# Head sums over squares split into two reduced-precision parts, and the hand-over from merge to routing without waits for stores

## The chip, the cores and the metric

The kernel runs on one core of a Trainium2 chip. The core has a matrix engine (TensorE, PE in the tables, with its weight loads as PEld), a vector engine (VectorE, DVE), an activation engine (ScalarE, ACT), a general engine (GpSimd, POOL) and a queue engine (SyncE, SP) that issues most transfers. The metric is the device time of one execution in microseconds; less is better.

## What is computed

One hybrid decoder block over 2048 tokens and 16 learned meta tokens (2064 columns), width 1024. Cut to what the change touches:

```python
xn = rmsnorm(h, norm1_g)
proj = xn @ w_in + b_in
u_conv, q, k, v, f_logit, gate_c, gate_a = split(proj)
y_conv = conformer_conv(u_conv, ...)
q = rmsnorm(q.reshape(B, L, N_HEADS, HEAD_DIM), q_norm_g)   # a sum over 64 channels of each head
k = rmsnorm(k.reshape(B, L, N_HEADS, HEAD_DIM), k_norm_g)
o = forgetting_attention(q, k, v, logf)
merged = sigmoid(gate_c) * y_conv + sigmoid(gate_a) * (o @ w_attn_out)
h = h + merged @ w_out
hn = rmsnorm(h, norm2_g)
h = h + hierarchical_moe(hn, ...)      # routing, then 64 experts of which each token takes 2
```

## The kernel before

The program is five stages, each a block of five instruction lists, one for each engine: project, attend, merge, route, experts. A block ends when every engine has come to its end, and only then does any engine start the next (the branch rows of L1326 and L1818 below are such a turning). All orders are written out by hand; engines wait on semaphores.

**Products in parts.** A matrix product of full-precision operands is made of three products of reduced-precision parts (type F32R): `pair_matmuls` (L92 to L94) multiplies high by high, low by high and high by low. A high part is a rounding copy, a low part the difference, made by an engine that subtracts.

**Project.** `w_in` is taken in tiles of 128 columns. PE makes a tile in five chunks of 412 or 414 of the 2064 columns (`CHUNKS`), 24 matmuls each, into banks 0 to 4. GpSimd splits the weight tile after next into its parts when PE has finished a tile (`split_w`, L396 to L403: a cast L400 and a subtraction L402). After 18 front tiles (convolution and gates) come `N_QK` = 8 tiles of queries and keys, 4 of values, one of the forget gate and further gates. In the 8 tiles of queries and keys each of the 40 chunks needs the mean square of its head: ScalarE reads the bank twice (L642, the scaled copy in `work`; L645, the square in `sq`), PE sums the squares over the channels of a head by a product with `head_ones` (`head_sum`, L501 to L510) after the chunk that follows, ScalarE takes the root (L626), VectorE the reciprocal (L830) and multiplies (L832), ScalarE makes the high part (L632) and VectorE the low part (L821) of the result. `head_ones` and `sq` are full-precision, so a head sum is one instruction, which the trace shows as two records. `sq`, `root` and `inv_root` have two buffers each. The last head sum follows right behind its own chunk (L515 and L516). At the start of the value tiles ScalarE and VectorE wait until all queries and keys are stored (L657, L840).

**Merge.** For each of four groups of 512 columns PE makes 8 products of the convolution and 8 of attention; VectorE gates and adds them (L1559, L1564, L1566) and SP stores each (L1400). In the last group ScalarE and VectorE also split `w_out` into parts, in 8 pieces: VectorE takes pieces 0 to 5 (`OUT_LOWS`, L1656), GpSimd pieces 6 and 7 (L1486 to L1488). SP's list ends with a wait for all eight stores (L1431 and L1432).

**Route.** 16 tiles of 128 tokens. For each, PE multiplies merged rows by `w_out` (48 matmuls), VectorE adds x (L2075), ScalarE and VectorE form the norm, PE turns the tile (L1911). GpSimd first makes eleven constants in a row (L1863 to L1881), and PE's list begins with a wait for the eleventh (L1902), although the first use is the first turning of a tile. Before tile 0 may be added, VectorE has to make `r_lo` (L2068) from what ScalarE makes at L2000, and that waits for five small transfers which SP issues behind the first rows, the gain `norm2_g` last. Rows of merged values for tile 2 are loaded once tile 0 has been added; their low part is L2344.

## Time and profile before

| what | value |
|---|---|
| median of 3 runs | 2595.53 us |
| lowest and highest | 2595.42, 2598.49 us |
| the profiled execution | 2595.53 us |
| its span in the trace | 2593.9 us |
| PE busy | 2450.6 us, 94% |
| DVE busy | 1839.8 us, 71% |
| ACT busy | 1049.9 us, 40% |
| POOL busy | 527.8 us, 20% |

The span is the stretch between the first and the last instruction in the trace; 1.6 us of the execution lie around it. Busy shares are means over stages with different limits, so the stage in question has to be looked at. A row of the timeline gives the start and the length of an instruction in microseconds from the span's start, and in brackets how long its engine had been idle and what ended that. Matmuls are pipelined: one shows as 0.35 us long where the next starts 0.19 us later, so PE's pace is read from starts.

### The profile page before, as it was taken

To read this page: it belongs to the slowest core of one execution; us is meant where nothing else is said; L and a number is where in the kernel's file an instruction comes from. 1 tells how busy PE (TensorE), PEld (TensorE's weight loads), DVE (VectorE), ACT (ScalarE), POOL (GpSimd) and SP (SyncE) were. 2 spreads that over 40 slices of the span, in tenths; PEclk is the share of its full clock that TensorE was granted. 3 is DMA by queue.
4 is the path that set the end of the run, shared out by engine and by line. 5 is a ranking of instruction groups with operands and counts; after the bars stand their busy time and mean duration, and the time that the engine had idled before them with its cause. 6 is when DMAs were issued, how large, how long until landed. Compare 5 with 4: busy or idle time off the path is not lost. (4 is left out here: it accounts for less than half of the span.)

```text
span 2593.9 us, 33454 instructions
## 1 busy us (share of the span) xinstructions
PE 2450.6 (94%) x12296; PEld 2002.8 (77%) x12296; DVE 1839.8 (71%) x2380; ACT 1049.9 (40%) x1516; POOL 527.8 (20%) x478
## 2 busy tenths in 40 slices
PE   6999999999999999999995998999399999999998
PEld 6899898999987878889884776877367767777664
DVE  7699999677211078888886775466588888888773
ACT  6101001443212168778774122233255555555540
POOL 1222222111101101111110001011324444232321
PEclk9999999999999999999998999999699999999999
DMA  5111212232325153364424776446379999999986
GB/s 173 41 57 57 68 54 68 71 123 82 108 103 157 49 149 100 100 171 110 115 82 123 204 224 224 178 148 227 138 293 357 368 375 360 372 370 370 361 315 199
DMA packets 180271, 469.84 MB, mean 181 GB/s; under 512 B 33573, under 2 KB 104579, under 8 KB 145548
## 3 DMA queue, kind: packets, MB, share of 16 engines
q1 hardware_dynamic: 133202, 371.64, 42.1%
q0 software_dynamic: 31120, 49.48, 5.6%
q10 hardware_dynamic: 15794, 46.67, 4.7%
q8 instruction: 96, 1.57, 0.2%
q14 instruction: 59, 0.48, 0.1%
HBM read 408.65 MB, written 118.29 MB: 203 GB/s over the span
## 5 line engine op out<-in xcount | busy, mean ns | idle before, releaser
L92 PE MATMUL project_bank<-project_xnT_hi,project_w_hi 128*128 128x512 f32 (+4 forms) x1352 | 511.3, 378 | 0.8 <-DVE project_work L788 0.7
L93 PE MATMUL project_bank<-project_xnT_lo,project_w_hi 128*128 128x512 f32 (+4 forms) x1352 | 497.4, 368 | 0.0
L94 PE MATMUL project_bank<-project_xnT_hi,project_w_lo 128*128 128x512 f32 (+4 forms) x1352 | 495.4, 366 | 0.0
L801 DVE SCALAR_TENSOR_TENSOR project_work<-project_work,project_taps 128x2048 f32<-128x2048 f32 x128 | 335.4, 2620 | 4.5
L92 PEld LDWEIGHTS project_bank<-project_xnT_hi,project_w_hi 128*128 128x128 f32 (+1 forms) x1352 | 250.6, 185 | 36.0 <-issue 7.7
L93 PEld LDWEIGHTS project_bank<-project_xnT_lo,project_w_hi 128*128 128x128 f32 (+1 forms) x1352 | 250.6, 185 | 32.5 <-issue 6.1
L94 PEld LDWEIGHTS project_bank<-project_xnT_hi,project_w_lo 128*128 128x128 f32 (+1 forms) x1352 | 250.7, 185 | 26.7
L2711 PE MATMUL experts_y_bank<-weights_down,experts_hT 128*128 128x512 f32 x544 | 246.4, 596 | 0.6 <-ACT experts_hT L2764 0.6
L1279 DVE TENSOR_TENSOR attend_pT<-attend_t_bank,attend_pT 128x512 fp32r<-128x512 f32 (+3 forms) x352 | 213.9, 614 | 33.7 <-ACT attend_pT L1213 32.8
L1146 PE MATMUL attend_o_bank<-attend_pT,attend_values 128*128 128x256 f32 x1216 | 225.2, 304 | 6.6 <-DVE attend_pT L1279 6.6
L92 PE MATMUL experts_gu_bank<-weights_high,experts_xT_hi 128*128 128x512 f32 x512 | 215.9, 422 | 6.9 <-DVE weights_low L2354 4.4
L1213 ACT ACTIVATE attend_pT<-attend_t_bank 128x512 fp32r<-128x512 f32 (+3 forms) x352 | 184.6, 540 | 87.3 <-PE attend_t_bank L1132 84.7
L93 PE MATMUL experts_gu_bank<-weights_low,experts_xT_hi 128*128 128x512 f32 x512 | 203.3, 397 | 0.0
L592 ACT ACTIVATE project_work<-project_bank,project_params 128x512 f32<-128x512 f32 x64 | 44.0, 690 | 393.4 <-PE project_bank L94 393.4
L94 PE MATMUL experts_gu_bank<-weights_high,experts_xT_lo 128*128 128x512 f32 x512 | 202.4, 395 | 0.0
L2354 DVE TENSOR_TENSOR weights_low<-weights_room,weights_high 128x2048 fp32r<-128x2048 f32 x86 | 193.0, 2285 | 0.0
L1132 PE MATMUL attend_t_bank<-first_ident,attend_probs 128*128 128x128 f32 x1216 | 191.0, 273 | 0.6 <-DVE attend_pT L1279 0.5
L400 POOL CAST project_w_hi<-project_w_raw 128x1024 fp32r<-128x1024 f32 (+1 forms) x35 | 46.5, 1330 | 706.3 <-PE project_bank L94 706.3
L2711 PEld LDWEIGHTS experts_y_bank<-weights_down,experts_hT 128*128 128x128 f32 x544 | 103.4, 191 | 105.7 <-issue 99.2
L2753 ACT ACTIVATE experts_xT_hi<-experts_x_bank 128x1024 fp32r<-128x1024 f32 x64 | 65.7, 1027 | 274.3 <-PE experts_x_bank L2672 219.2
L1146 PEld LDWEIGHTS attend_o_bank<-attend_pT,attend_values 128*128 128x128 f32 x1216 | 167.8, 190 | 9.2 <-DVE attend_pT L1279 8.6
L2349 ACT ACTIVATE weights_high<-weights_room 128x2048 fp32r<-128x2048 f32 x86 | 164.0, 1909 | 13.2 <-DMA weights_room<-in_w_up_dram 13.1
(316 smaller groups left out, 4624.4 us busy)
## 6 DMA issues: line engine op xcount, KB each, us to landing
weights_down<-in_w_down_dram SPq DMA_DIRECT2D x68, 1024.0 KB
weights_room<-in_w_gate_dram SPq DMA_DIRECT2D x45, 1024.0 KB
weights_room<-in_w_up_dram SPq DMA_DIRECT2D x45, 1024.0 KB
weights_third<-in_w_gate_dram SPq DMA_DIRECT2D x23, 1024.0 KB
weights_third<-in_w_up_dram SPq DMA_DIRECT2D x23, 1024.0 KB
project_w_raw<-in_w_in_dram SPq DMA_DIRECT2D x36, 512.0 KB, 4.2
qk_d<-project_work SPq DMA_DIRECT2D x16, 1032.0 KB, 5.4
gate_d<-project_work ACTq DMA_DIRECT2D x16, 1024.0 KB, 4.2
```

What stands on the lines that cost most here:

```text
L92: pe.matmul(out, lhs[0], rhs[0], start=first, stop=False)
L93: pe.matmul(out, lhs[0], rhs[1], start=False, stop=False)
L94: return pe.matmul(out, lhs[1], rhs[0], start=False, stop=last)
L801: nc.vector.scalar_tensor_tensor(out=work[:, 2, 0:SEQ], in0=work[:, 1, META - 1 + q:META - 1 + q + SEQ], scalar=taps[:, bass.ds(ct, 1), q] ...
L1132: m = nc.tensor.transpose(t_bank[:, j % 3, (t % 4) * P:(t % 4 + 1) * P], probs[:, u % BUF, t * P:(t + 1) * P], ident[:, :])
L1146: m = nc.tensor.matmul(out, values[:, h, t, :], pT[:, j % (LAG + 1), t % 4].rearrange("p k q -> p (k q)"), start=t == 0, stop=t == last)
L1213: nc.scalar.activation(pT[:, j % (LAG + 1), 0:n, 0, :], t_bank[:, j % 3, 0:n * P].rearrange("p (t q) -> p t q", q=P), ACT.Copy)\
L1279: nc.vector.tensor_tensor(pT[:, j % (LAG + 1), 0:n, 1, :], t_bank[:, j % 3, 0:n * P].rearrange("p (t q) -> p t q", q=P), raw(pT[:, j % (LA ...
L2349: nc.scalar.activation(self.high[n % 2][:, cut, :, :].rearrange("p c k n -> p k c n"), self.gate_up_rooms[n % 3][:, :, cut, :], ACT.Copy)\
L2354: nc.vector.tensor_tensor(self.low[n % 2][:, cut, :, :].rearrange("p c k n -> p k c n"), self.gate_up_rooms[n % 3][:, :, cut, :], raw(self ...
L2711: m = nc.tensor.matmul(y_bank[:, b, half, :], hT[:, b, c, :], down_raw[r][:, c, cols], start=c == 0, stop=c == HC - 1)
L2753: nc.scalar.activation(xT_hi[:, b, :, :], x_bank[:, :, :].rearrange("p k (c t) -> p (k c) t", t=P), ACT.Copy).then_inc(x_hi_ready, 1)
```

## The change

1. **Head sums.** ScalarE writes the square twice, in full precision (`sq`) and as its high part (`sq_hi`). GpSimd subtracts (`low_squares`, 40 new instructions on 412 or 414 columns, five ahead of each split of a weight tile), and a head sum is two F32R matmuls with `pair_ones`, over the high and the low part. PE waits for GpSimd's part (`sq_lo_ready`). `sq` and `root` have one buffer now, `inv_root` is gone: the reciprocal is made in place, ScalarE's next square waits for the subtraction, its next root for VectorE's product.
2. **The last head sum** stands between the first and the second chunk of the first value tile.
3. **Start of the value tiles.** VectorE doesn't wait for the stores there, ScalarE waits for them where it first writes in their place.
4. **Merge's end.** SP's waits for the stores go to where they are needed: in route on VectorE (ahead of its first writes in that memory) and on SP ahead of the load of tile 12. VectorE takes piece 6 of `w_out` in merge and piece 7 as its first instruction of route; GpSimd takes none.
5. **Constants.** PE waits for the eleven constants ahead of its first turning of a tile instead of at the start of its list.

Two memory tiles of route (`onehot`, `places`) change places in memory.

```diff
@@ -407,12 +414,22 @@
...
-            for it in range(0, N_QK // 2):
-                for b in range(2):
-                    split_w(it * 2 + (N_FRONT + b), b, it + (N_FRONT // 2 + 1))
-            for it in range(0, N_V // 2):
-                for b in range(2):
-                    split_w(it * 2 + (N_FRONT + N_QK + b), b, it + ((N_FRONT + N_QK) // 2 + 1))
+            def low_squares(n):
+                for i, (at, size) in enumerate(CHUNKS):
+                    g = 5 * n + i
+                    wait(pool, bank_read[i], (N_FRONT if i < 4 else 2 * CT) + n + 2)
+                    if g >= 2:
+                        wait(pool, sum_ready, g - 1)
+                    nc.gpsimd.tensor_tensor(sq_lo[:, g % 2, 0:size], sq[:, 0:size], raw(sq_hi[:, g % 2, 0:size]),
+                                            ALU.subtract).then_inc(sq_lo_ready, 1)
+
+            for n in range(2):
+                split_w(N_FRONT + n, n, N_FRONT // 2 + 1)
+            for n in range(N_QK):
+                low_squares(n)
+                split_w(N_FRONT + n + 2, n % 2, (N_FRONT + n) // 2 + 2)
+            for n in range(2, N_V):
+                split_w(N_FRONT + N_QK + n, n % 2, (N_FRONT + N_QK + n) // 2 + 1)
...
@@ -497,23 +514,19 @@
...
+            def head_sum(g):
+                r, size = g % 2, CHUNKS[g % 5][1]
+                pe.wait_ge(root2_ready, g + 1)
+                pe.wait_ge(sq_lo_ready, g + 2)
+                nc.tensor.matmul(bank[:, 5 + r, 0:size], pair_ones[:, :], sq_hi[:, r, 0:size],
+                                 start=True, stop=False)
+                nc.tensor.matmul(bank[:, 5 + r, 0:size], pair_ones[:, :], sq_lo[:, r, 0:size],
+                                 start=False, stop=True).then_inc(sum_ready, 1)
...
             def pair_tile(it, b):
-                def head_sum(g):
-
-
-                    i, r = g % 5, g % 2
-                    size = CHUNKS[i][1]
-
-                    pe.wait_ge(bank_read[i], it * 2 + ((N_FRONT if i < 4 else 2 * CT) + g // 5 + 2))
-                    pe.wait_ge(root2_ready, it * 10 + (g + 1))
-                    nc.tensor.matmul(bank[:, 5 + r, 0:size], head_ones[:, :], sq[:, r, 0:size],
-                                     start=True, stop=True).then_inc(sum_ready, 1)
-
-                first = isinstance(it, int) and it == 0 and b == 0
-                project(it * 2 + (N_FRONT + b), b, CHUNKS, (it * 2 + (N_FRONT + b), it * 2 + (2 * CT + b)),
-                        between=lambda i: None if first and i == 0 else head_sum(5 * b + i - 1))
-                if isinstance(it, int) and it * 2 + b == N_QK - 1:
-                    head_sum(9)
+                n = it * 2 + b
+                project(N_FRONT + n, b, CHUNKS, (N_FRONT + n, 2 * CT + n),
+                        between=lambda i: head_sum(5 * n + i - 1) if n or i else None)
...
                 project(N_FRONT + N_QK + n, n % 2, CHUNKS, (N_FRONT + N_QK + n, 2 * CT + N_QK + n),
-                        between=(lambda g: turn_values(n - 1, g)) if n else None)
+                        between=lambda g: turn_values(n - 1, g) if n else head_sum(5 * N_QK - 1) if g == 0 else None)
...
@@ -622,8 +635,9 @@
                 def root_of(g):
                     r, size = g % 2, CHUNKS[g % 5][1]
                     wait(act, sum_ready, it * 10 + (g + 1))
-                    wait(act, inv_ready, it * 10 + (g + 1))
-                    nc.scalar.activation(root[:, r, 0:size], bank[:, 5 + r, 0:size], ACT.Sqrt,
+                    if it * 10 + g:
+                        wait(act, qn_ready, it * 10 + g)
+                    nc.scalar.activation(root[:, 0:size], bank[:, 5 + r, 0:size], ACT.Sqrt,
                                          bias=eps[:, 0:1], scale=1.0 / HD).then_inc(root2_ready, 1)
...
@@ -642,7 +656,10 @@
                     nc.scalar.activation(work[:, 0, at:at + size], bank[:, i, 0:size], ACT.Identity,
                                          bias=gain_bias[:, bass.ds(it * 2 + b, 1)],
                                          scale=gain[:, bass.ds(it * 2 + b, 1)])
-                    nc.scalar.activation(sq[:, g % 2, 0:size], bank[:, i, 0:size], ACT.Square,
+                    wait(act, sq_lo_ready, it * 10 + (g + 1))
+                    nc.scalar.activation(sq[:, 0:size], bank[:, i, 0:size], ACT.Square,
+                                         bias=bias[:, bass.ds(it * 2 + (8 + b), 1)])
+                    nc.scalar.activation(sq_hi[:, g % 2, 0:size], bank[:, i, 0:size], ACT.Square,
                                          bias=bias[:, bass.ds(it * 2 + (8 + b), 1)]).then_inc(bank_read[i], 1)
...
             over_pair_tiles(pair_tile)
-            for s in qk_stored:
-                wait(act, s, 16 + 16 * N_QK)
+            wait(act, q_lo_ready, 5 * N_QK + 5)
             wait(act, v_pad_ready, 2)
...
                 if g == 0:
                     wait(act, v_stored[n % 2], n // 2 * 16 + 16)
+                    if n < 2:
+                        wait(act, qk_stored[n], 16 + 16 * N_QK)
                 wait(act, v_turned, 5 * n + g + 1)
...
@@ -825,20 +842,17 @@
                 dve.wait_ge(qk_stored[b], it * 32 + 16)
                 for i, (at, size) in enumerate(CHUNKS):
                     g = 5 * b + i
-                    r = g % 2
                     dve.wait_ge(root2_ready, it * 10 + (g + 3))
-                    nc.vector.reciprocal(inv_root[:, r, 0:size], root[:, r, 0:size]).then_inc(inv_ready, 1)
-                    dve.wait_ge(inv_ready, it * 10 + (g + 3))
+                    nc.vector.reciprocal(root[:, 0:size], root[:, 0:size]).then_inc(inv_ready, 1)
+                    dve.wait_ge(inv_ready, it * 10 + (g + 1))
                     nc.vector.tensor_tensor(work[:, 0, at:at + size], work[:, 0, at:at + size],
-                                            inv_root[:, r, 0:size], ALU.mult).then_inc(qn_ready, 1)
+                                            root[:, 0:size], ALU.mult).then_inc(qn_ready, 1)
...
             over_pair_tiles(pair_tile)
-            for s in qk_stored:
-                dve.wait_ge(s, 16 + 16 * N_QK)
             dve.wait_ge(q_lo_ready, 5 * N_QK + 5)
...
@@ -1428,8 +1442,6 @@
                 wait(sp, s, 32)
             next_weights.load_merged(sp, merged_d, 0, 0)
             chunk(TC - 1, False, False)
-            for s in m_stored:
-                wait(sp, s, 16 + 16 * TC)
...
@@ -1483,9 +1495,6 @@
         def _(pool):
             wait(pool, next_weights.merged_hi_ready, 1)
             next_weights.low_merged(nc.gpsimd, 0)
-            for k in range(OUT_LOWS, DC):
-                wait(pool, next_weights.out_hi_ready, k + 1)
-                next_weights.low_out(nc.gpsimd, k, next_weights.out_lo_ready2)
...
-OUT_LOWS = 6
+OUT_LOWS = 7
...
                 sp.dma_start(halves[:, k * size:(k + 1) * size], empty).then_inc(table_cleared, 16)
             for n in range(2, NT):
+                if n == NT - NT // TC:
+                    for s in first_weights.merged_stored:
+                        wait(sp, s, 16 + 16 * TC)
                 load_tile(n, n % 2)
-            wait(sp, r_lo_ready, OUT_LOWS + 1)
+            wait(sp, r_lo_ready, DC + 1)
...
 
         @block.tensor
         def _(pe):
-            pe.wait_ge(consts_ready, 11)
-
             def turn(c, j):
 
                 n = c * CHUNK + j
+                if n == 0:
+                    pe.wait_ge(consts_ready, 11)
                 pe.wait_ge(hn_ready, n + 1)
                 if n < NT - 1:
...
             def low_m(c, j):
                 wait(dve, m_hi_ready, c * CHUNK + (j + 1))
                 first_weights.low_merged(nc.vector, j % 2)
+
+            for k in range(OUT_LOWS, DC):
+                wait(dve, first_weights.out_hi_ready, k + 1)
+                first_weights.low_out(nc, k)
+            for s in first_weights.merged_stored:
+                wait(dve, s, 16 + 16 * TC)
```

On PE, between the second and third chunk of the first tile of queries, before (`project_extra` holds `sq`):

```order
L94 MATMUL project_bank<-project_xnT_hi,project_w_lo 128x412
L509 MATMUL project_bank<-project_extra,project_head_ones 128x412 [waits project_root2_ready,project_bank_read1]
L92 MATMUL project_bank<-project_xnT_hi,project_w_hi 128x414 [waits project_bank_read3]
L93 MATMUL project_bank<-project_xnT_lo,project_w_hi 128x414
L94 MATMUL project_bank<-project_xnT_hi,project_w_lo 128x414
```

and now:

```order
L94 MATMUL project_bank<-project_xnT_hi,project_w_lo 128x412
L521 MATMUL project_bank<-project_squares,project_pair_ones 128x412 [waits project_sq_lo_ready,project_root2_ready]
L523 MATMUL project_bank<-project_squares,project_pair_ones 128x412
L92 MATMUL project_bank<-project_xnT_hi,project_w_hi 128x414 [waits project_bank_read3]
L93 MATMUL project_bank<-project_xnT_lo,project_w_hi 128x414
L94 MATMUL project_bank<-project_xnT_hi,project_w_lo 128x414
```

One full-precision instruction became two, and the wait is for GpSimd's part instead of ScalarE's read of the bank. On GpSimd nothing stood between two splits of weight tiles before; at the same place of the program there is now (`project_squares` holds both parts of the squares):

```order
L423 TENSOR_TENSOR project_squares<-project_extra,project_squares 128x414 [waits project_sum_ready,project_bank_read4]
L407 CAST project_w_hi<-project_w_raw 128x1024 [waits project_tile_done,project_w_loaded0]
L409 TENSOR_TENSOR project_w_lo<-project_w_raw,project_w_hi 128x1024 [waits project_w_hi_ready]
L423 TENSOR_TENSOR project_squares<-project_extra,project_squares 128x412 [waits project_sum_ready,project_bank_read0]
L423 TENSOR_TENSOR project_squares<-project_extra,project_squares 128x412 [waits project_sum_ready,project_bank_read1]
```

The split of the weight tile stands behind the last of five subtractions. On PE at the turning from merge to route, before:

```order
L93 MATMUL merge_y_bank<-merge_o_lo,merge_wm_hi 128x512
L94 MATMUL merge_y_bank<-merge_o_hi,merge_wm_lo 128x512
L1326 UNCONDITIONAL_BRANCH
L1900 UNCONDITIONAL_BRANCH [waits barrier_Pool_Activation_PE_DVE_SP_release]
L92 MATMUL route_h_bank<-weights_high,weights_merged_hi 128x512 [waits route_h_ready,weights_out_lo_ready,weights_merged_lo_ready,route_consts_ready]
L93 MATMUL route_h_bank<-weights_low,weights_merged_hi 128x512
```

and now:

```order
L93 MATMUL merge_y_bank<-merge_o_lo,merge_wm_hi 128x512
L94 MATMUL merge_y_bank<-merge_o_hi,merge_wm_lo 128x512
L1340 UNCONDITIONAL_BRANCH
L1912 UNCONDITIONAL_BRANCH [waits barrier_Pool_Activation_PE_DVE_SP_release]
L92 MATMUL route_h_bank<-weights_high,weights_merged_hi 128x512 [waits weights_out_lo_ready,route_h_ready,weights_merged_lo_ready]
L93 MATMUL route_h_bank<-weights_low,weights_merged_hi 128x512
```

The wait for the constants is gone from the first product of route; on VectorE `low_out` for piece 7 now stands first in route, with the waits for the stores behind it.

## Rows read from the trace of the kernel before

**Rows 1.** Who PE waited for between 440 and 915 us: total, times, longest.

```profile
PE project_bank L509 <- ACT project_extra L645: 1.7, 2, 1.1
```

**Rows 2.** Timeline of PE around two head sums: start, length, line, tiles.

```profile
475.96 0.35 PE L94 MATMUL project_bank<-project_xnT_hi,project_w_lo 128*128 128x414 f32 x1
476.15 0.86 PE L509 MATMUL project_bank<-project_extra,project_head_ones 128*128 128x414 f32 x2
...
477.04 0.35 PE L93 MATMUL project_bank<-project_xnT_lo,project_w_hi 128*128 128x412 f32 x1
...
481.35 0.86 PE L509 MATMUL project_bank<-project_extra,project_head_ones 128*128 128x414 f32 x2
```

**Rows 3.** Timeline of the other engines in the same chunk.

```profile
476.41 0.70 ACT L642 ACTIVATE project_work<-project_bank,project_gain_bias,project_gain 128x414 f32<-128x414 f32 x1 [3.06 <-PE project_bank L94]
476.45 1.24 POOL L400 CAST project_w_hi<-project_w_raw 128x1024 fp32r<-128x1024 f32 x1 [22.49 <-PE project_bank L94]
...
477.01 0.60 ACT L645 ACTIVATE project_extra<-project_bank,project_params 128x414 f32<-128x414 f32 x1
...
477.50 0.60 ACT L626 ACTIVATE project_extra<-project_bank,project_eps 128x414 f32<-128x414 f32 x1
...
477.77 2.40 POOL L402 TENSOR_TENSOR project_w_lo<-project_w_raw,project_w_hi 128x1024 fp32r<-128x1024 f32 x1
...
478.13 2.74 DVE L830 RECIPROCAL project_extra<-project_extra 128x414 f32<-128x414 f32 x1 [1.34 <-ACT project_extra L626]
...
480.91 0.59 DVE L832 TENSOR_TENSOR project_work<-project_work,project_extra 128x414 f32<-128x414 f32 x1
```

**Rows 4.** Timeline of ScalarE at the first chunk of queries.

```profile
459.19 0.69 ACT L642 ACTIVATE project_work<-project_bank,project_gain_bias,project_gain 128x412 f32<-128x412 f32 x1 [8.15 <-DVEq L812]
```

**Rows 5.** Timeline of PE around the last head sum.

```profile
658.17 0.35 PE L94 MATMUL project_bank<-project_xnT_hi,project_w_lo 128*128 128x414 f32 x1
...
660.85 0.35 PE L93 MATMUL project_bank<-project_xnT_lo,project_w_hi 128*128 128x412 f32 x1
```

**Rows 6.** Groups of instructions, shapes apart: busy us, mean ns, idle before.

```profile
L1095 POOL TENSOR_TENSOR attend_o_sb<-attend_o_raw 128x128 f32<-128x128 f32 x128 | 57.5, 470 | 396.3 <-ACT attend_o_raw L1221 348.4 <-DMA o_d<-attend_o_sb 47.9
```

**Rows 7.** VectorE's additions in merge (ns, least, median, most), and GpSimd's timeline.

```profile
L1566 DVE TENSOR_TENSOR merge_m_sum<-merge_m_sum,merge_prod_a x32: 691/692/1957, 1433.4 to 1599.5; 128x512 f32<-128x512 f32 x32
...
1595.40 5.48 POOL L2337 TENSOR_TENSOR weights_low<-weights_room,weights_high 128x1024 fp32r<-128x1024 f32 x2 [21.91 <-ACT weights_high L2334]
```

**Rows 8.** Timeline of SP at the turning from merge to route.

```profile
1594.74 7.06 SPq L1400 DMA_DIRECT2D merged_d<-merge_m_sum  x3
1604.20 0.35 SPq L1821 DMA_DIRECT2D weights_down<-in_x_dram  x1
```

**Rows 9.** Timeline of PE in route's first three tiles.

```profile
1608.77 0.80 PE L92 MATMUL route_h_bank<-weights_high,weights_merged_hi 128*128 128x512 f32 x1 [10.13 <-POOL route_lane L1880]
...
1632.65 1.04 PE L1911 MATMUL route_t_bank<-route_ident,route_hn_sb 128*128 128x128 f32 x8
1633.44 0.47 PE L92 MATMUL route_h_bank<-weights_high,weights_merged_hi 128*128 128x512 f32 x1
```

**Rows 10.** Timeline of ScalarE and VectorE there.

```profile
1617.01 0.69 ACT L2000 ACTIVATE route_r_hi<-weights_room 128x576 fp32r<-128x576 f32 x1 [6.81 <-DMA weights_gain<-in_norm_g_dram]
...
1621.96 1.23 DVE L2075 TENSOR_TENSOR route_h_sb<-route_h_bank,weights_down 128x1024 f32<-128x1024 f32 x1 [3.48 <-PE route_h_bank L94]
...
1630.34 1.23 DVE L2344 TENSOR_TENSOR weights_merged_lo<-weights_merged_lo,weights_merged_hi 128x1024 fp32r<-128x1024 f32 x1 [2.30 <-ACT weights_merged_hi L2340]
```

**Rows 11.** The turning from project to attend: ScalarE's last, SP's and PE's first.

```profile
915.30 0.37 ACTq L596 DMA_DIRECT2D gate_d<-project_work  x1
...
917.03 0.61 SPq L1056 DMA_DIRECT2D attend_values<-v_d  x1
...
917.41 0.42 PE L1117 MATMUL attend_s_bank<-first_half 128*128 128x400 f32 x1 [2.94 <-DVEq L1257]
```

**Rows 12.** Busy time by engine, granted clock (PEclk), transfers in route's first 4 us.

```profile
1608.77:1612.80 4.03, 4.03 (x10) 3.24 (x11) 1.23 (x1) 1.06 (x1) 0.21 (x1) 0.52 0.76 182
```

35 lines of the change are left out of this document (19 added, 16 removed).

## Prediction

> **What bounds the kernel now.** I read the waits of PE first, for the stretch that the change touches. Between 440 and 915 us PE waited for other engines 1.7 us in all, twice, both for a head sum [rows 1]: in project PE alone sets the time, and whatever PE no longer does there is gained, as long as its feeders keep up. Then the timeline of PE around two head sums [rows 2]: they start 5.20 us apart (476.15, 481.35), which is the period of a chunk. Then the other engines in the same chunk [rows 3]: VectorE has 1.34 us idle before each reciprocal, so it is the second limit and not far away. The second place is the turning from merge to route, read from the timelines of SP, PE, ScalarE and VectorE [rows 8 to 10]: PE stands 10.13 us, by the row for GpSimd's eleventh constant. Attend, the other groups of merge and the experts are not touched; each stage starts when the one before has ended on all engines, so what is gained here shifts them and nothing more.
>
> **Part 1, the 38 ordinary head sums.** From the chunk's last L94 to the L93 of the next chunk lie 1.08 us (475.96 to 477.04) [rows 2]. Without a head sum these would be two steps of a chunk's pace. A step is (5.20 − x)/24, with x the cost of a head sum, and 1.08 = x + two steps: x = 0.71, step 0.187. Now two reduced-precision matmuls of the same width stand there, at the same step: 0.37. Saved: 0.33 (0.71 − 0.37, unrounded) × 38 = 12.7 us, a chunk's period becomes 4.87.
>
> Do the feeders keep 4.87? Take T as the end of a chunk on PE, 0.35 behind the start of its last matmul: 476.31 in rows 2. **ScalarE** [rows 3]: L642 starts at T + 0.1, L645 0.60 later, the next 0.49 later. With the second square (priced as L645, 0.60) the high part is there at T + 0.1 + 0.60 + 0.49 + 0.60 = T + 1.8, the root starts at T + 1.7 and ends at T + 2.3. ScalarE's five steps are issued in some 2.7 of 4.87 us. **GpSimd**: the trace has no subtraction on 412 columns. Nearest rows: 0.47 on 128 columns [rows 6] and 2.40 on 1024 [rows 3]; on the line between them 1.08. It ends at T + 2.9, PE asks at T + 4.5 (behind the next chunk's 24 steps). Ends of the unknown: 0.47 costs nothing; 2.40 ends at T + 4.3 and costs nothing in the middle of a tile, but at the 7 passages to a next tile the split (1.24 + 2.40) comes in between, until T + 8.0, and the next subtraction ends at T + 10.4, where PE asks at T + 9.4: 7 us lost. I take 1.08; then the split ends at T + 6.6, before the next high part at T + 6.7. Behind it in GpSimd's list waits only the weight tile after next, which has four chunks to spare. **VectorE** [rows 3]: reciprocal 2.74, product 0.59, low part about the same, 3.9 of 4.87 us. The one-buffered root makes a ring, root 0.60, reciprocal 2.74, product 0.59, with hand-overs some 4.1: also below 4.87. The reciprocal runs from T + 2.3 to 5.0, the product ends at T + 5.6, the next root is due at T + 6.6.
>
> **Here a rule speaks against the change.** In merge, VectorE's addition of two operands in memory took 0.69 us in the median and 1.96 at most, and the last of them, begun at 1599.5, ran while GpSimd subtracted beside it until 1600.9 [rows 7]. The Trainium skill, GPSIMD Engine Reference, section "8. Key points", says it in general: GpSimd shares its interfaces to memory with VectorE, and contends with VectorE's instructions that have two inputs there; by it the product and the low part are exposed, and the sum below would lose rival B's amount, 8 us. Against that, the reciprocal with its one input ran 2.74 us with GpSimd's subtraction (477.77 to 480.17) all along it [rows 3]. By the times above the short subtractions (T + 1.8 to 2.9) lie beside the reciprocal, and only the split, once in five chunks, reaches the product (T + 4.2 to 6.6 against T + 5.0 to 6.2). That delays one root by some 0.6 us, which the next chunk's idle 1.0 us takes back; PE doesn't feel it, since it needs the roots two chunks later. Cost 0.
>
> **The first head sum** waits longer: ScalarE's first chunk starts at 459.19 [rows 4]; the high part ends at 459.19 + 0.60 + 0.49 + 0.60 = 460.9, GpSimd's part at 462.0. PE waited 1.1 us for it before and started at about 460.4; now 1.6 later, less 0.33: +1.3 us. **The last** [rows 5]: 658.17 to 660.85 are 2.68 us, two steps off it 2.31; between value chunks there is nothing to wait for (GpSimd's part is at T + 2.9, PE asks at T + 4.5), so it costs 0.37: −1.9. ScalarE and VectorE then finish the last chunk about 1 us later than before, but the wait for the stores is gone; PE needs the first bank back only five chunks, over 20 us, later. GpSimd's one more small copy at the start (`pair_ones`) stands ahead of its first split of a weight tile, which has the loading of x as its cover. Project: −12.7 + 1.3 − 1.9 = **−13.3 us**, with the unknown subtraction between −13.9 and −5.
>
> **Part 2, the turning.** SP's last store ends at 1594.74 + 7.06 = 1601.80, and SP starts in route at 1604.20 [rows 8]; the landing lies between. VectorE's last addition began at 1599.5, and with GpSimd's split beside it I take the longest time, 1.96, for it [rows 7]. Without that split it takes 0.69 and ends at 1600.2; the store is issued by 1600.6. How long a turning takes without a landing to wait for: from project to attend 915.67 to 917.03 = 1.4 us, PE's first matmul 0.4 behind SP [rows 11]; the lower end is 0.5, what is left of 1601.80 to 1604.20 if the landing took 1.9. I take 0.9: SP starts at 1601.5, 2.7 earlier, PE at 1601.7, 7 us earlier. What is late next? PE's tiles 0 and 1 take 1608.77 to 1632.65 = 23.9 us before [rows 9]. In the first 4 us the granted clock was 0.52, near the 1.2 GHz level, and PE did 10 matmuls [rows 12], which costs 1.8 us against the later pace of 0.23. From project to attend PE had been idle 2.94 us [rows 11] and the attend matmuls behind started at full pace; here it would be idle 1601.7 − 1598.7 = 3.0. I take it that the clock stays: tiles 0 and 1 end at 1601.7 + 22.1 = 1623.8, turned at 1624.6. The constants are needed only there, over 20 us in. But the other chain moves with SP's start only: ScalarE has the gain and so the router's high part at 1617.01 − 2.7 = 1614.3, VectorE adds tile 0 at 1617.01 + 0.69 + 0.7 − 2.7 = 1615.7 instead of 1621.96 (0.7 for L2068: 576 of the 1024 columns for which L2344 takes 1.23), and from that addition to the end of tile 2's low part are 1631.57 − 1621.96 = 9.6 us [rows 10]: 1625.3. So tile 2 starts at 1625.3 instead of 1633.44 [rows 9]: **−8.1 us**; a further gain on PE's side would be lost on this chain. Behind it VectorE has 2 to 3 us to spare in a tile, as before. The waits for stores that VectorE gets cost nothing: the last store lands about 1603, VectorE's next work, behind them in its list, waits for tile 1's rows anyway, which SP only asks for at 1602. Piece 7 of `w_out`, 1.2 us as VectorE's first step, is needed by PE's 22nd matmul, 5 us in. Bounds: turning 0.5 and a quicker chain of small transfers −9.9; turning 1.4 and a low clock again −6.5.
>
> **Sum.** −13.3 − 8.1 = −21.4 on the profiled execution's 2595.53 us, which is also the median: **2574.1 us**. Own range 2571 to 2578.
>
> **Rivals.**
> A. *The clock falls at the turning all the same.* Tiles 0 and 1 end 1.8 later, at 1626.4 with the turning of the tile, against the chain's 1625.3: 1.1 lost, 2575.2. Inside the forecast's range.
> B. *VectorE's two-input steps stand still while GpSimd works* (the rule above, with phases that drift together). At most one short subtraction a chunk: 3.9 + 1.1 = 5.0 against 4.87, 0.13 × 33; and at the 7 passages the rest of a split, up to 1.6 us, of which 1.0 is idle time: 4 + 4 us given back, 2582. For: the 1.96 us rows. Against: the phases above.
> C. *VectorE stands still for all that GpSimd does, and becomes the bound* (the other side). GpSimd works 5 × 1.08 + 3.64 = 9.0 us a tile, 1.8 a chunk; 3.9 + 1.8 = 5.7 against today's 5.20: +0.5 × 40 = +20, + 1.3 − 1.9 − 8.1: 2607. It makes the kernel slower once VectorE's time in a chunk passes 5.4. Against it the reciprocal's row, which was not slowed.
> D. *PE waits for GpSimd at each passage* (subtraction near 2.4 us): 7 us given back, with the first wait 1.3 more: 2582. For it only that no row has this width; against it the line between two rows.
> E. *Merge's part doesn't do what it says*: another engine or transfer ends the turning as late as before, SP starts at 1604.2; only the 10.1 us wait shrinks, and the chain holds tile 2 at 1628.0: 5.4 gained instead of 8.1, 2577. For it: the landing of that store is the only thing the trace shows as waited for; what stood behind it can't be seen.
>
> **How the numbers follow.** The forecast with A 0.76, E 0.06, B 0.06, D 0.05, C 0.02, a gain past the forecast's end 0.02, a loss of most of the gain by something not listed 0.03. About 0.2% (5 us) is what a measurement of this kernel can tell from no change. Faster: all but C and the last, 0.95; same 0.03; slower 0.02. For 8 in 10 the range takes the forecast, A and E and the near side of B and D: 2569.5 to 2580.
>
> **What would show it.** Right: head sums of two rows 0.19 us apart, a chunk's period of 4.87 (PE busy throughout), one wait of some 2.7 us at the first head sum and none at the last, VectorE's reciprocal still 2.7 us with about 1 us idle before it; at the turning PE idle 3 us, SP's first transfer about 0.9 us behind its last store, and a short wait (under 1 us) before tile 2. Wrong: products on VectorE (0.59 now) of over 1 us in many chunks (B), PE waiting for `project_squares` (D), reciprocals of over 3 us (C), SP starting as late behind VectorE's last addition as before (E), a chain of small transfers in route that doesn't move with SP's start.

## The result, and the profile after

The changed kernel took 2578.27 us in the median of 4 runs (2577.1 to 2585.55), against 2595.48 of the kernel before beside it (2592.07 to 2598.49): a ratio of 0.9944, 95% interval 0.9924 to 0.9963. It is faster, as foreseen. But the forecast was a gain of 21.4 us, and the ratio gives 14.5 (2581.0, a little outside the range's end of 2580; the two medians alone differ by 17.2). In two more comparisons, below, the ratios were 0.9922 and 0.9945. All medians taken together, 2579.0 of 14 runs against 2595.9 of 47, give 16.9 us. So 4 to 5 us of the forecast are missing.

The profiled execution of the changed kernel is the slowest of its four (2585.55, span 2583.9). Its total is therefore no guide, but its stages are. I line the two traces up by a row that the change doesn't touch: ScalarE's reading of the third of the four chunks of the last front tile, before and after (a timeline: start, length, line, tiles, idle time before):

```profile
444.79 0.69 ACT L592 ACTIVATE project_work<-project_bank,project_params 128x512 f32<-128x512 f32 x1 [4.87 <-PE project_bank L94]
```

```profile
447.53 0.69 ACT L605 ACTIVATE project_work<-project_bank,project_params 128x512 f32<-128x512 f32 x1 [4.87 <-PE project_bank L94]
```

After was 2.7 us late here already; of the change only one small copy on GpSimd (`pair_ones`) and moved memory lie ahead of this row. I call the time from this row to PE's first matmul of attend "project": it holds the 8 tiles of queries and keys and what follows them. It was 472.62 us before (917.41 in [rows 11] less 444.79) and is 909.63 − 447.53 = 462.10 after, 10.5 less:

```profile
909.63 0.67 PE L1131 MATMUL attend_s_bank<-first_half 128*128 128x400 f32 x1 [2.93 <-DVEq L1271]
```

Who PE waited for between 440 and 905 us, answering to [rows 1]:

```profile
engine line waited for: us in total, times, longest us
PE project_bank L521 <- POOL project_squares L423: 2.7, 1, 2.7
```

PE's timeline at that one wait, the first head sum, and in two windows around it (length, PE busy, granted clock, share of the DMA engines, GB/s):

```profile
464.79 0.53 PE L521 MATMUL project_bank<-project_squares,project_pair_ones 128*128 128x412 f32 x1 [2.71 <-POOL project_squares L423]
465.12 0.55 PE L523 MATMUL project_bank<-project_squares,project_pair_ones 128*128 128x412 f32 x1
465.46 0.55 PE L92 MATMUL project_bank<-project_xnT_hi,project_w_hi 128*128 128x412 f32 x1
```

```profile
440.00:470.00 30.00, 27.29 (x125) 0.94 0.27 88
470.00:900.00 430.00, 430.00 (x2190) 1.00 0.30 100
```

The matmuls behind the wait start 0.34 us apart and not 0.19: the granted clock was at its lower level, 1.2 GHz, for a few microseconds, hence the mean of 0.94 of 2.4 GHz in the first window. After that PE is busy for all of 430 us. The last head sum, which answers to [rows 5], shows the pair 0.18 us apart:

```profile
657.01 0.34 PE L521 MATMUL project_bank<-project_squares,project_pair_ones 128*128 128x414 f32 x1
657.19 0.35 PE L523 MATMUL project_bank<-project_squares,project_pair_ones 128*128 128x414 f32 x1
```

The other engines at a passage to a next weight tile, where GpSimd has the split and the subtraction (timelines of GpSimd and of VectorE, to compare with [rows 3]):

```profile
485.23 2.41 POOL L409 TENSOR_TENSOR project_w_lo<-project_w_raw,project_w_hi 128x1024 fp32r<-128x1024 f32 x1
487.98 0.92 POOL L423 TENSOR_TENSOR project_squares<-project_extra,project_squares 128x412 fp32r<-128x412 f32 x1 [0.34 <-ACT project_squares L662]
```

```profile
483.53 2.74 DVE L846 RECIPROCAL project_extra<-project_extra 128x414 f32<-128x414 f32 x1 [1.01 <-ACT project_extra L640]
486.31 1.78 DVE L848 TENSOR_TENSOR project_work<-project_work,project_extra 128x414 f32<-128x414 f32 x1
488.01 1.33 DVE L838 TENSOR_TENSOR project_work<-project_work 128x412 fp32r<-128x412 f32 x1
489.26 2.73 DVE L846 RECIPROCAL project_extra<-project_extra 128x414 f32<-128x414 f32 x1
492.02 0.59 DVE L848 TENSOR_TENSOR project_work<-project_work,project_extra 128x414 f32<-128x414 f32 x1
```

Beside GpSimd's split the product takes 1.78 us instead of 0.59, and the low part behind it (L838), which begins just after GpSimd's next subtraction, 1.33 instead of 0.58; all 40 reciprocals take 2.73 to 2.74. The two steps are 1.9 us longer together. The next reciprocal follows without idle time (489.26), and the one after it has 0.31 us (493.42) instead of 1.01. One chunk later the product is at 0.59 again, and PE never noticed.

At the turning from merge to route, PE's last matmul of merge before and after, then SP's timeline, PE's, and VectorE's (to [rows 7 to 10]):

```profile
1598.26 0.39 PE L94 MATMUL merge_y_bank<-merge_o_hi,merge_wm_lo 128*128 128x512 f32 x1
```

```profile
1593.60 0.39 PE L94 MATMUL merge_y_bank<-merge_o_hi,merge_wm_lo 128*128 128x512 f32 x1
```

```profile
1590.08 5.80 SPq L1414 DMA_DIRECT2D merged_d<-merge_m_sum  x3
1596.29 0.34 SPq L1830 DMA_DIRECT2D weights_down<-in_x_dram  x1
```

```profile
1596.48 0.47 PE L92 MATMUL route_h_bank<-weights_high,weights_merged_hi 128*128 128x512 f32 x1 [2.49 <-DVEq L2052]
1618.95 1.03 PE L1923 MATMUL route_t_bank<-route_ident,route_hn_sb 128*128 128x128 f32 x8
1619.74 0.47 PE L92 MATMUL route_h_bank<-weights_high,weights_merged_hi 128*128 128x512 f32 x1
```

```profile
1594.81 0.69 DVE L1575 TENSOR_TENSOR merge_m_sum<-merge_m_sum,merge_prod_a 128x512 f32<-128x512 f32 x1
1618.02 1.23 DVE L2360 TENSOR_TENSOR weights_merged_lo<-weights_merged_lo,weights_merged_hi 128x1024 fp32r<-128x1024 f32 x1 [2.01 <-ACT weights_merged_hi L2356]
```

SP starts 0.4 us behind its last store (1595.88 to 1596.29), PE is idle 2.49 us instead of 10.13 and runs straight through its first two tiles. I call the time from the start of PE's last matmul of merge to the start of its first of tile 2 "the turning": 1598.26 to 1633.44 = 35.18 us before, 1593.60 to 1619.74 = 26.14 after, 9.0 less. VectorE's low part of tile 2 is there at 1619.25, just ahead of PE.

This table has the same lengths for all kernels of this study, from one profiled execution each (us). "Front" is the time of ScalarE's row above; attend runs to PE's first matmul of merge, merge from there to its last; the rest runs from tile 2 to the span's end.

| kernel | front | project | attend | merge | turning | rest |
|---|---|---|---|---|---|---|
| before | 444.8 | 472.6 | 475.8 | 205.0 | 35.2 | 960.5 |
| after | 447.5 | 462.1 | 478.3 | 205.6 | 26.1 | 964.2 |
| e1_again | 444.5 | 462.1 | 476.0 | 205.2 | 27.7 | 959.1 |
| e2_heads | 444.5 | 462.1 | 476.6 | 204.8 | 36.1 | 956.7 |
| e3_turning | 446.8 | 472.7 | 477.6 | 205.3 | 26.1 | 956.9 |
| e4_late_first | 445.8 | 457.8 | 477.8 | 204.7 | 26.1 | 956.6 |
| e5_constants | 444.5 | 472.7 | 477.6 | 203.9 | 31.5 | 955.8 |
| e6_stores | 444.4 | 472.7 | 475.8 | 204.6 | 32.9 | 959.8 |
| e7_pool_split | 446.7 | 472.6 | 477.6 | 203.6 | 30.3 | 957.9 |
| e8_double_sub | 446.8 | 469.4 | 477.7 | 203.7 | 27.7 | 956.8 |
| e9_last_only | 445.0 | 471.7 | 477.6 | 204.4 | 36.1 | 959.4 |
| e10_long_wait | 447.4 | 475.4 | 476.0 | 204.4 | 36.2 | 957.3 |
| e11_late_first2 | 444.5 | 457.8 | 476.5 | 205.3 | 26.1 | 961.1 |
| e12_again2 | 447.6 | 462.0 | 477.8 | 205.9 | 25.9 | 958.2 |

Project repeats to 0.1 us in every execution of the same code, and the turning comes in steps. The stages that the change doesn't touch vary by 2 to 8 us. What an edit is worth is read from its own stage; the total only confirms it.

### The profile page after: what moved, and what is told of

Its sections match the earlier page's. It is cut to its first block and busy times, and to the rows that moved or that the text cites. A ratio compares the mean times of both kernels' runs of the same rounds, so it can differ in the third digit from the quotient of the medians.

```text
span 2583.9 us, 33571 instructions
## 1 busy us (share of the span) xinstructions
PE 2447.0 (95%) x12296; PEld 2008.5 (78%) x12296; DVE 1852.7 (72%) x2382; ACT 1071.7 (41%) x1556; POOL 563.0 (22%) x517
## 5 line engine op out<-in xcount | busy, mean ns | idle before, releaser
L92 PE MATMUL project_bank<-project_xnT_hi,project_w_hi 128*128 128x512 f32 (+4 forms) x1352 | 500.1, 370 | 0.7 <-DVE project_work L806 0.6
L1146 PEld LDWEIGHTS attend_t_bank<-first_ident,attend_probs 128*128 128x128 f32 x1216 | 148.6, 140 | 25.2 <-issue 3.9
## 6 DMA issues: line engine op xcount, KB each, us to landing
weights_third<-in_w_up_dram SPq DMA_DIRECT2D x23, 1024.0 KB, 14.5
```

The source lines that it names most:

```text
L92: pe.matmul(out, lhs[0], rhs[0], start=first, stop=False)
L1146: m = nc.tensor.transpose(t_bank[:, j % 3, (t % 4) * P:(t % 4 + 1) * P], probs[:, u % BUF, t * P:(t + 1) * P], ident[:, :])
```

## Experiments on the two parts

**The whole, and each part alone.** The kernel with the first part has all of the diff that lies in project; the other has all that lies in merge and route.

> The changed kernel once more, beside the three kernels that hold parts of it. Theory M (the mechanism is right, two terms are off in size: the head sums gain about 10.5 and the turning 9, some 19.5 in all, and the rest of the shortfall of the first result is the spread of executions): median 2576 +- 1.5. Rival V (the change really gains only the 14 to 17 us of the first interval because attend and the experts lose 2 to 4.5 us behind it): median 2579 to 2581. If the forecast were right after all: 2574. In the profile, a first head sum of project that waits 2.7 us with matmuls of about 0.54 behind it for some 3 us, if the low clock there belongs to the change and not to that one execution.

Measured: 2575.30 us median (5 runs, 2573.92 to 2579.26), ratio 0.9922 (0.9906 to 0.9939) against 2596.66. The wait of 2.7 us and the low clock are there again (0.94 from 440 to 470 us), so they belong to the change.

> The kernel before with the first part of the change alone: the split squares, GpSimd's subtractions, the last head sum between value products, no waits for stores at project's end. Forecast of the prediction for this part: -13.3, so 2582.2. Theory M: -10.5 (12.7 + 1.9 saved, 1.3 lost to the longer first wait, 1.7 lost to the low clock behind it, and about 1 because a chunk's period is 4.89 and not 4.87), so 2585. Rival V: less than -9. PE from its first head sum to the last one takes 40 periods of 4.89; the turning from merge to route stays as before, with PE's wait of 10.1 us.

Measured: 2584.84 us, ratio 0.9959 (0.9944 to 0.9975); project 462.10, which is −10.5 to the digit.

> The kernel before with the second part alone: merge's end without waits for stores, pieces 6 and 7 of w_out on VectorE, the constants waited for at the first turning. Forecast of the prediction: -8.1, so 2587.4. Theory M: -9.0, so 2586.5, with PE idle about 2.5 us at the turning and the router's chain just in time for tile 2. Rival E (something else ends the turning as late): -5.4. If the two parts are independent, the gains of this kernel and of the one with the head sums alone add up to that of the changed kernel, within 1.5 us.

Measured: 2586.55 us, ratio 0.9962 (0.9947 to 0.9977); turning 26.14, −9.0. The medians' gains, 11.8 and 10.1, add up to 21.9, against 21.4 for the whole in the same comparison: the parts add up. In the stages it is 10.5 and 9.0. The whole turned in 27.7 us in e1_again, and a window at the start of route says why; e1_again first, after behind it:

```profile
1590.71:1600.00 9.29, 9.29 (x33) 0.82 0.87 250
```

```profile
1596.48:1605.80 9.32, 9.32 (x40) 1.00 0.85 245
```

With the same idle time of 2.5 us the clock fell to its lower level for part of the stretch in one execution and not in the other: 33 matmuls instead of 40, 1.56 us (27.70 − 26.14).

**The halves of the turning.** First the constants' wait alone:

```
     @block.tensor
-            pe.wait_ge(consts_ready, 11)
             def turn(c, j):
+                if n == 0:
+                    pe.wait_ge(consts_ready, 11)
```

> The kernel before with one edit: TensorE waits for GpSimd's constants at its first turning and not at its start. TensorE then starts 0.4 us behind SyncE's first transfer of route, some 4.2 us earlier than before (6 us idle instead of 10.1). Theory M (two chains meet at tile 2, and the later one decides): tiles 0 and 1 take 22.1 to 23.9 us, so tile 2 starts 4.2 to 5.4 us earlier, bound by the chain from the gain to tile 0's addition, which doesn't move: gain 4 to 5.4. Rival: the other chain (ScalarE's gain, the router's parts) was the bound of tile 2 all along, gain under 1; or the start of the stage counts fully, gain as large as 7.

Measured: 2594.44 us (10 runs), ratio 0.9989 (0.9978 to 1.0001), inconclusive by itself. In the stage: turning 31.54, 3.6 us less than the 35.18 of before, 4.6 less than the 36.1 that three other kernels with the old turning show. PE's first matmul of route:

```profile
1605.54 0.77 PE L92 MATMUL route_h_bank<-weights_high,weights_merged_hi 128*128 128x512 f32 x1 [6.49 <-DVEq L2043]
```

Next, everything of the second part but that edit:

> The kernel before with the rest of the second part: no waits for stores at the end of merge and no piece of w_out on GpSimd, but TensorE still waits for all constants at its start. Theory M: SyncE starts about 0.4 us behind its last store (before: 2.4), but TensorE then waits for the eleventh constant, which GpSimd writes 5.5 us behind its own start: 7 to 8 us idle, and tile 2 starts 2.0 to 3.3 us earlier. Then neither half alone gives the 9.0 of both, and the two halves about add up (4 to 5.4 and 2 to 3.3; more than 8.7 in sum if the clock stays full only in one of them). Rival: the store waits alone bring nearly all (8 to 9) and the constants were no more than the visible name of the wait.

Measured: 2592.89 us (10 runs), ratio 0.9991 (0.9981 to 1.0001), again inconclusive; turning 32.88, 2.3 to 3.3 less. SP issued 0.4 us behind its last store (1599.38 + 0.36 to 1600.14), but PE stood for the constants; SP's and PE's rows:

```profile
1599.38 0.36 SPq L1400 DMA_DIRECT2D merged_d<-merge_m_sum  x1
1600.14 0.35 SPq L1816 DMA_DIRECT2D weights_down<-in_x_dram  x1
```

```profile
1605.76 0.80 PE L92 MATMUL route_h_bank<-weights_high,weights_merged_hi 128*128 128x512 f32 x1 [7.93 <-POOL route_lane L1878]
```

Alone the two halves give 3.6 and 2.3, both at once 9.0, so 3.1 more than their sum. Of these 1.4 are the clock: it fell behind idle times of 6.49 and 7.93 us, and TensorE took 24.6 to 24.7 us for the two tiles (24.67 in before); behind 2.49 us it stayed up in `after` and they took 23.26. The other 1.8 are idle time: the halves shorten PE's 10.13 us by 3.6 and 2.2, both by 7.6, because each half alone leaves the other's wait standing in part.

**What the two pieces of `w_out` on GpSimd cost.** Stores and constants as in the changed kernel, but the pieces stay on GpSimd and VectorE takes neither (+ marks what the kernel with the second part lacks; the edits on VectorE and PE that go with it aren't shown):

```
         @block.gpsimd (merge)
             next_weights.low_merged(nc.gpsimd, 0)
+            for k in range(OUT_LOWS, DC):          # OUT_LOWS = 6
+                wait(pool, next_weights.out_hi_ready, k + 1)
+                next_weights.low_out(nc.gpsimd, k, next_weights.out_lo_ready2)
```

> The kernel before with waits for stores moved and the constants' wait moved, but pieces 6 and 7 of w_out stay on GpSimd, where they stand at merge's end. The prediction held VectorE's last addition for lengthened by GpSimd's split beside it (up to 1.96 us against 0.69). If so: that addition takes 1.0 to 2.0 us again, GpSimd's split of piece 7 ends 2 us or more behind TensorE's last matmul of merge, the stage turns only behind it, and tile 2 starts 0.7 to 2 us later than with both pieces off GpSimd (gain 7 to 8.3 instead of 9.0). Rival: GpSimd's split takes nothing from VectorE and ends in time: gain 9.0 as with the whole second part.

Measured: 2587.18 us, ratio 0.9968 (0.9951 to 0.9985); turning 30.27, so 4.9 less than before and 4.1 more than with the whole second part, twice the most that was expected. GpSimd's and VectorE's timelines at the end of merge, and PE's first matmul of route:

```profile
1596.80 2.42 POOL L2342 TENSOR_TENSOR weights_low<-weights_room,weights_high 128x1024 fp32r<-128x1024 f32 x1 [20.89 <-ACT weights_high L2339]
1599.71 2.81 POOL L2342 TENSOR_TENSOR weights_low<-weights_room,weights_high 128x1024 fp32r<-128x1024 f32 x1 [0.49 <-ACT weights_high L2339]
```

```profile
1596.88 3.42 DVE L2342 TENSOR_TENSOR weights_low<-weights_room,weights_high 128x1024 fp32r<-128x1024 f32 x1
1600.23 0.68 DVE L1562 TENSOR_TENSOR merge_prod_a<-merge_y_bank,merge_room 128x512 f32<-128x512 f32 x1
1600.94 2.13 DVE L1564 TENSOR_TENSOR merge_m_sum<-merge_m_sum,merge_prod_a 128x512 f32<-128x512 f32 x1
1602.99 0.68 DVE L1562 TENSOR_TENSOR merge_prod_a<-merge_y_bank,merge_room 128x512 f32<-128x512 f32 x1
1603.70 0.69 DVE L1564 TENSOR_TENSOR merge_m_sum<-merge_m_sum,merge_prod_a 128x512 f32<-128x512 f32 x1
```

```profile
1605.38 0.77 PE L92 MATMUL route_h_bank<-weights_high,weights_merged_hi 128*128 128x512 f32 x1 [4.49 <-DVEq L2044]
```

PE in the 7.6 us behind it, and in a window of the same length in route's first tile in the kernel after:

```profile
1605.40:1613.00 7.60, 7.60 (x23) 0.67 0.96 279
```

```profile
1605.40:1613.00 7.60, 7.60 (x34) 1.00 0.92 351
```

VectorE's own piece takes 3.42 us beside GpSimd's (in the kernel after the same size takes 1.22) and an addition with both operands in memory 2.13 instead of 0.69, while `L1562`, which reads one operand from the accumulation banks, keeps its 0.68. By that VectorE ends merge 3.9 us behind PE's last matmul (1604.39 against 1600.50) instead of 1.9 (1595.50 against 1593.60), and so PE is idle 4.49 us instead of 2.49. What the extra time is can be read from the two timelines: VectorE's piece ran beside GpSimd's for 2.34 us (1596.88 to 1599.22) and took 2.20 longer, its addition for 1.58 us (1600.94 to 1602.52) and took 1.44 longer. GpSimd's second piece, begun at 1599.71 while VectorE's ran until 1600.30, took 2.81 instead of 2.42. In each pair the one that began second stood still until the first was done, less 0.1 to 0.2 us. Here the clock fell (23 matmuls where the kernel after has 34), and the two tiles took 25.39 us and not 23.26, which is the other half. The prediction named the effect, but priced it at 1.3 us on one addition.

**How much cover GpSimd's subtraction has.**

```
                     nc.gpsimd.tensor_tensor(sq_lo[...], sq[...], raw(sq_hi[...]),
-                                            ALU.subtract).then_inc(sq_lo_ready, 1)
+                                            ALU.subtract).then_inc(sq_first, 1)
+                    wait(pool, sq_first, g + 1)
+                    nc.gpsimd.tensor_tensor(sq_lo[...], sq[...], raw(sq_hi[...]),
+                                            ALU.subtract).then_inc(sq_lo_ready, 1)
```

> The changed kernel with every subtraction of GpSimd's done twice, so that the low part comes 1.1 to 1.2 us later. It prices the rival that TensorE waits for GpSimd where the split of a weight tile comes in between. Working with the changed kernel's times: the high part is there 1.8 us behind a chunk's end, the doubled subtraction ends at 4.1, TensorE asks at 4.5: nothing lost inside a tile. At the 7 passages the split (1.04 + 2.40) follows until 7.7, the next doubled subtraction ends at 9.9 to 10.2, TensorE asks at 9.4: 0.5 to 0.8 lost at each, 3.5 to 5.6 in sum; the first head sum waits 1.2 longer. Together +4.7 to +7 against the changed kernel. If GpSimd stood in VectorE's way beyond that (rivals B and C), reciprocals would be over 3 us and the period of a chunk over 4.89 everywhere: +10 or more. If GpSimd's part has more cover than worked out here: +1.2 alone.

Measured: 2583.85 us (4 runs), ratio 0.9952 (0.9936 to 0.9969); the totals are too coarse for it (the changed kernel had 0.9922 to 0.9945). Project is 469.38, +7.3 against the changed kernel. PE's waits from 440 to 905 us, and one passage on PE:

```profile
PE project_bank L525 <- POOL project_squares L427: 7.2, 8, 3.8
```

```profile
487.38 0.35 PE L525 MATMUL project_bank<-project_squares,project_pair_ones 128*128 128x414 f32 x1
492.95 0.42 PE L525 MATMUL project_bank<-project_squares,project_pair_ones 128*128 128x412 f32 x1 [0.50 <-POOL project_squares L427]
```

One wait at the first head sum and one at each of the 7 passages, as worked out; none inside a tile. The sum lies a little above the 4.7 to 7 that were expected: the longer first wait brought another 1.0 us of low clock (7.53 us from the first head sum to the second, 6.51 in the changed kernel), which had been left out. The reciprocals stayed at 2.73 us, and the chunks between passages at 4.87 to 4.90 (4.98 for the one right behind a passage). In the changed kernel the subtraction behind a split ended at 488.90 (the row above), and PE asked for it here:

```profile
490.85 0.35 PE L521 MATMUL project_bank<-project_squares,project_pair_ones 128*128 128x412 f32 x1
```

That is a cover of 1.95 us. Doubling used it up with twice the 1.1 us (the subtraction ahead of the split counts too) and some 0.4 by which the split itself became longer (2.78). So I estimate that rival D decides from a subtraction of about 1.8 us on (1.05 and half of 1.95 − 0.4), and rival C isn't near even with the subtractions doubled.

## Experiments on project's missing 2.8 us

**Is the wait at the first head sum to be had?** The changed kernel with one edit in PE's list:

```
-                        between=lambda i: head_sum(5 * n + i - 1) if n or i else None)
+                def sums(i):
+                    if n or i > 2:
+                        head_sum(5 * n + i - 1)
+                    elif i == 2:
+                        head_sum(0)
+                        head_sum(1)
```

> The changed kernel, but the head sum of the first chunk is issued behind the third chunk, together with that of the second, so that PE has no reason to wait for ScalarE and GpSimd at the first chunk. Theory M: the wait of 2.7 us goes, and with it the low clock behind it (some 1.7 us): 3 to 4.4 us less than the changed kernel, so about 2572, and PE's matmuls at the start of the query and key tiles take 0.36 throughout. Rival 1: the clock falls there for another reason (the long stretch before it, or the heat of the chip) and only the wait goes: -2.7. Rival 2: the wait only moves, because ScalarE is now a root behind and VectorE's chain of 4.1 us a chunk takes the cover away: 0 to -1, with waits of PE at later head sums of the first tile.

Measured: 2570.84 us (5 runs, 2570.43 to 2578.24), ratio 0.9911 (0.9894 to 0.9929), on the same chip as e1_again's 2575.30. PE's two windows:

```profile
440.00:470.00 30.00, 30.00 (x148) 1.00 0.27 88
470.00:900.00 430.00, 430.00 (x2184) 1.00 0.30 100
```

PE is busy for all of it. Project is 457.80, so 4.3 less: 2.7 of wait and 1.6 of clock. The rivals fall: the clock doesn't fall there for another reason, and the wait doesn't move.

**Is it the wait that lets the clock fall?** The kernel before, with three copies on ScalarE that nothing reads, ahead of the first square:

```
+                    if first and i == 0:
+                        for idle in (inv_root[:, 0, 0:size], inv_root[:, 1, 0:size], root[:, 1, 0:size]):
+                            nc.scalar.activation(idle, bank[:, i, 0:size], ACT.Copy)
                     nc.scalar.activation(sq[:, g % 2, 0:size], bank[:, i, 0:size], ACT.Square,
```

> The kernel before with three more copies of the first query chunk on ScalarE, into places that nothing reads, ahead of its square. TensorE's wait at the first head sum becomes about 2.6 us (1.1 and three times 0.5) with nothing else changed: no split square, no GpSimd subtraction. Theory M (it is the length of the wait that lets the clock fall): the granted clock from 440 to 470 us is 0.94 as in the changed kernel, and project is 1.5 + 1.5 = 3.0 us longer than the 472.6 of before. Rival (the clock fell for the new form of the head sum, or for other work beside it): the clock stays 1.00 and project is 1.5 us longer.

One run, read by its stage: PE waited 2.29 us (the copies came 0.39 apart), the granted clock from 440 to 470 us was 0.94, and project took 475.44, +2.8: 1.2 of wait and 1.6 of clock. PE's row and the window:

```profile
464.25 1.68 PE L509 MATMUL project_bank<-project_extra,project_head_ones 128*128 128x412 f32 x2 [2.29 <-ACT project_extra L648]
```

```profile
440.00:470.00 30.00, 27.70 (x124) 0.94 0.27 88
```

So neither the split squares nor GpSimd is needed for it. In this place a wait of 1.1 us left the clock alone in every trace, and waits of 2.3, 2.7 and 3.8 us lowered it in every trace.

**What was the last head sum worth?** The kernel before, the last head sum, still of full precision, issued behind the first value chunk (the body of `last_head_sum`, its waits and the same matmul, isn't shown):

```
-                if isinstance(it, int) and it * 2 + b == N_QK - 1:
-                    head_sum(9)
...
-                        between=(lambda g: turn_values(n - 1, g)) if n else None)
+                        between=lambda g: turn_values(n - 1, g) if n else last_head_sum() if g == 0 else None)
```

> The kernel before with one edit: the last head sum, still one full-precision matmul, stands behind the first value chunk. It asks what the prediction's term for the last head sum (-1.9) was worth by itself. In the kernel before, 658.36 to 660.66 us holds two head sums and a wait of 0.65. Theory M (the term counted the head sum in front of the last one twice): from 2.30 us, 0.69 stays for that one and 0.69 comes back between the value chunks, so attend starts 0.9 us earlier against project's first convolution than before (472.62), and the change's own last term is -1.2 and not -1.9. Rival (the term was right and the missing 0.7 us lies elsewhere): 1.6 earlier. The total time of one run can't tell these apart; the stage's length in the profile can (it was 472.6 in all kernels with the old head sums).

One run, read by its stage: project 471.72, −0.9 as for a term that counts a head sum twice (1.6 if it didn't), and the wait of 0.65 us between the rows of [rows 5] is gone.

**Once more, side by side.** The kernel of e4_late_first and the changed kernel:

> The kernel with the postponed first head sum once more, beside the changed kernel, for the size of its lead. By the stage boundaries of its first profile: project 4.3 us shorter than in the changed kernel (457.8 against 462.1), everything behind as before, so 4.3 us (0.17%) less than the changed kernel and 24 less than before, about 2572. If the first comparison (25.8 less than before) was luck, 2575 or more.

> The changed kernel once more, as the neighbour of the run above. By stages: project -10.5, turning -9.0 in executions with full clock behind it and -7.5 in those where it falls: -18 to -19.5, so 2577 to 2579 where before is 2596.5. If the true gain is the forecast's 21.4: 2575.

Measured: 2574.24 us (6 runs), ratio 0.9920 (0.9907 to 0.9932), and 2580.99 us (5 runs), ratio 0.9945 (0.9932 to 0.9958). Project was 457.81 and 462.03. The version with the postponed first head sum beats both kernels: over both comparisons 2572.3 (11 runs), some 23.6 us below before. The changed kernel came out 2 us above the upper end expected of it.

## Why the prediction was right and where it was wrong

**Right: the mechanism.** In project PE alone sets the time, the head sums became two rows 0.19 us apart, one wait of 2.7 us stands at the first and none at the last, VectorE keeps 1.0 us idle before a reciprocal, and GpSimd's subtraction on 412 columns takes 1.05 us in the mean, where the line between two rows gave 1.08. Its place, T + 1.8 to 2.9, held, as e8_double_sub confirms from the other side. At a passage VectorE lost 1.9 us and not 0.6, because the low part was hit as well as the product; the idle time of two chunks took that back instead of one's.

**Wrong: project gained 10.5 and not 13.3.** Two steps failed. The term for the first head sum priced the longer wait and put the clock behind it at nothing, without a reason; the term for the last head sum saved a head sum that the first term had saved already. Term by term:

- *38 ordinary head sums, −12.7.* Measured −12.1. The mean period of a chunk went from 5.205 to 4.887. The step is 0.188 (4.887/26) and the old head sum 0.694, where two rows gave 0.187 and 0.71; an error of 0.016 us times 38 is 0.6.
- *The last, −1.9.* Measured −1.2. The 2.31 us between the rows of [rows 5] held two head sums, the one before the last among them, and that one was also counted among the 38. A double count of 0.7, visible in the rows themselves; e9_last_only gives 0.9 for the move alone, and the split adds 0.3.
- *The first, +1.3.* The wait was right (1.6 longer). What was left out is the clock behind it: +1.5 to 1.6. The prediction weighed a falling clock at the turning (rival A) and didn't ask the same question at the wait that it had itself lengthened from 1.1 to 2.7 us.

−12.1 − 1.2 + 1.3 + 1.5 = −10.5.

**The turning: −8.1 forecast, −9.0 or −7.5 measured.** The turnover took 0.4 us and not 0.9 (the range's lower end was 0.5), so PE was idle 2.5 and not 3.0. PE follows SP by 0.2 us, the figure that the sum used, though its text says 0.4. The chain that was to hold tile 2 at 1625.3 came in time. On the time axis of before (4.66 us later) its low part is there at 1623.9 and tile 2 starts at 1598.26 + 26.14 = 1624.4. So PE's side decided, and rival A came true in some executions: with the same idle time the clock stayed in five traces (after, e3, e4, e11, e12) and fell in two (e1, e8), which costs the full 1.6 us and not 1.1. The forecast took it from one row, attend's first, that the clock stays up behind 2.94 us. That one trace was luck: PE is idle 2.93 to 2.97 us there in all fourteen, and the granted clock of attend's first 3.4 us was 1.00 in seven of them and 0.50 to 0.74 in the other seven, `after` among them (PE's windows of before and of after):

```profile
917.41:920.81 3.40, 3.04 (x14) 1.00 1.00 283
```

```profile
909.63:913.03 3.40, 3.40 (x9) 0.50 0.98 285
```

Against the 36.1 us that three of the four kernels with the old turning show, the gain is 8.4 to 10.2. The sum was nearly right for partly wrong reasons, and that is luck. The turnover was priced too dear. With the pieces left on GpSimd two prices would have been missing, VectorE's own split of 3.42 us beside GpSimd's and the clock behind a longer idle time (e7_pool_split).

**The rivals.** *B*: the standstill exists. The rule that was weighed, in the Trainium skill, GPSIMD Engine Reference, section "8. Key points", is borne out by this case: at the passages the product takes 1.78 us instead of 0.59, and merge's additions 2.13 instead of 0.69; the reciprocal with its one input was not touched. VectorE pays where it begins second; where it begins first, GpSimd does (2.81 and 2.78 us instead of 2.4). What the forecast said of it held too, that PE wouldn't feel it in project. The total alone, near 2581 in two comparisons, would have fitted this rival's 2582; the traces exclude it, since PE has no wait in project but the first and a chunk's period stays at 4.89. *C* and *D*: no trace of either; e8_double_sub shows from where D would count. *E*: didn't happen, but e5_constants and e6_stores show how near it is: with either half missing, 5.4 to 6.7 of the 9.0 us stay away.

**What stays open.** By the stages, the changed kernel should gain 18 to 20 us; the pooled medians give 16.9 (17.2, 21.4 and 14.8 in the three comparisons). In the three traces of its code, front, attend, merge and rest together took 2084.8, 2089.5 and 2095.7 us, in the eleven others 2081.8 to 2087.4. Front was at 447.5 in two of the three, and between 444.4 and 447.4 in the others; the rest reached 964.2 once. The two traces with the postponed first head sum, whose code in these stages is the same, took 2084.9 and 2087.4, which speaks for chance. So does the clock: behind tile 2 it was at its lower level for 60.7 us in `after`, for 56.2 in before and for 45.6 in e5_constants, and these stretches took 964.2, 960.5 and 955.8 us; a line through all fourteen traces gives 0.5 us for each us at the lower level. The most of that spread is the clock's, then. The other two traces of the changed code had 54.5 us each, inside the 45.6 to 57.8 of the rest. Why the clock differs from one execution to the next, and whether the change has a part in it, stays open.

## What to carry to other kernels

Read an edit's worth from its own stage, bounded by two events that the edit doesn't touch: here that repeated to 0.1 us while the total moved by 10. When a change makes TensorE wait longer, add the clock behind the wait to its price (here 1.5 to 1.6 us for a wait of over 2 us, as much as the lengthening itself), and look for a place a little later in TensorE's list where the same work needs no wait. Before a sum over "n ordinary ones and a special one", check that the interval measured for the special one doesn't hold an ordinary one.
